# Norm boundaries of a two-layer encoder ordered by sequence, with the means spread by a product with ones, and a quarter of the first modulation moved to the vector engine

## What is computed

```python
for i in range(2):
    mod = silu(c) @ w_mod[i] + b_mod[i]            # 6 x 1024 columns per sequence
    sh1, sc1, g1, sh2, sc2, g2 = split(mod, 6)
    h = rmsnorm(x, norm1_g[i]) * (1 + sc1) + sh1
    mix = even_mixer(h) if i % 2 == 0 else odd_mixer(h)
    x = x + g1 * mix
    h = rmsnorm(x, norm2_g[i]) * (1 + sc2) + sh2
    x = x + g2 * ((silu(h @ w_g) * (h @ w_u)) @ w_down)
return rmsnorm(x, final_g)
# rmsnorm(x, g) = x * rsqrt(mean(x * x over the 1024 features) + eps) * g
```

## Time and profile before

| | |
|---|---|
| median of 3 runs | 2123.8 us (2117.55 to 2126.86) |
| profiled execution, own time | 2124.51 us |
| its span | 2122.4 us |
| mean granted clock of PE | 0.967 of full |
| PE busy | 2017.7 us (95%) |
| VectorE busy | 992.6 us (47%) |
| ScalarE busy | 601.7 us (28%) |
| chain that ended last, by engine | PE 87%, DVE 6%, ACT 4%, issue 2%, DMA 1% |

### The profile page before, as it was taken

The page is one execution under the profiler, slowest core; times in us unless marked ns, Lnnn a source line. Parts: engine busy times, 40 slices in busy tenths (PEclk is TensorE's granted clock), DMA queues, the critical chain, the costliest instruction groups (busy, mean ns, idle before and its releaser), DMA issues.

```text
span 2122.4 us, 28746 instructions
## 1 busy us (share of the span) xinstructions
PE 2017.7 (95%) x12081; PEld 1742.5 (82%) x12081; DVE 992.6 (47%) x1875; ACT 601.7 (28%) x1101; POOL 74.3 (4%) x121
## 2 busy tenths in 40 slices
PE   7879999988899999999998999998989999999998
PEld 2768888767788888888887788888878888888887
DVE  1877425684766665652235334544452222222224
ACT  3235224652321112211223333334232211211213
POOL 2010000000011101100000000000000000000000
PEclk9889999999899999999998999999989999999999
DMA  7343112012344444432223201021212222222212
GB/s 282 120 150 108 41 41 80 21 31 60 99 142 138 136 122 139 142 96 60 65 62 104 60 20 41 21 99 49 61 50 60 60 70 60 64 66 60 62 56 82
DMA packets 210249, 174.16 MB, mean 82 GB/s; under 512 B 10320, under 2 KB 196792, under 8 KB 208584
## 3 DMA queue, kind: packets, MB, share of 16 engines
q1 hardware_dynamic: 197536, 117.67, 18.5%
q0 software_dynamic: 12288, 48.35, 7.1%
q10 hardware_dynamic: 296, 6.29, 0.7%
HBM read 162.85 MB, written 9.44 MB: 81 GB/s over the span
## 4 chain that ended last, share of the span: by engine, by line
PE 87%; DVE 6%; ACT 4%; issue 2%; DMA 1%; POOL 0%; ACTq 0%; DVEq 0%; POOLq 0%
PE bank L824 60%; PE bank L790 9%; PE bank L842 4%; PE bank L1096 2%; PE bank L747 1%; PE bank L765 1%; DMA early_raw<-in_w_mod_dram 1%; ACT w_hi L1221 1%; DVE early_acc L1620 1%; DVE w_lo L1601 1%; PE bank L1018 1%; PE bank L908 1%; PE bank L1041 1%; PE bank L966 1%; PE bank L1068 1%
## 5 line engine op out<-in xcount | busy, mean ns | idle before, releaser
L824 PE MATMUL bank<-h_hi,w_hi 128*128 128x256 f32 x1600 | 409.4, 338 | 0.1
L824 PE MATMUL bank<-h_lo,w_hi 128*128 128x256 f32 x1600 | 407.5, 336 | 0.0
L824 PE MATMUL bank<-h_hi,w_lo 128*128 128x256 f32 x1600 | 407.3, 336 | 0.0
L1601 DVE TENSOR_TENSOR w_lo<-raw,w_hi 128x1024 fp32r<-128x1024 f32 (+4 forms) x195 | 239.0, 1230 | 340.2 <-ACT w_hi L1221 340.1
L824 PEld LDWEIGHTS bank<-h_hi,w_lo 128*128 128x128 f32 x1600 | 301.3, 188 | 33.6
L824 PEld LDWEIGHTS bank<-h_lo,w_hi 128*128 128x128 f32 x1600 | 301.4, 188 | 33.2
L824 PEld LDWEIGHTS bank<-h_hi,w_hi 128*128 128x128 f32 x1600 | 299.4, 188 | 34.2 <-issue 1.9
L1221 ACT ACTIVATE w_hi<-raw 128x1024 fp32r<-128x1024 f32 (+4 forms) x196 | 205.6, 1053 | 226.3 <-DMA raw<-in_ffn_w_down_dram 129.1
L790 PE MATMUL bank<-w_hi,h_hi 128*128 128x256 f32 x672 | 214.8, 320 | 18.1 <-DVE w_lo L1601 17.7
L790 PE MATMUL bank<-w_lo,h_hi 128*128 128x256 f32 x672 | 195.8, 291 | 0.0
L790 PE MATMUL bank<-w_hi,h_lo 128*128 128x256 f32 x672 | 195.6, 291 | 0.0
(11 more groups left out here) (274 smaller groups left out, 2251.7 us busy)
## 6 DMA issues: line engine op xcount, KB each, us to landing
raw<-in_ffn_w_gu_dram SPq DMA_DIRECT2D x176, 256.0 KB, 3.3
late_raw<-in_w_mod_dram POOLq DMA_DIRECT2D x56, 512.0 KB, 4.3
raw<-in_ffn_w_down_dram SPq DMA_DIRECT2D x64, 256.0 KB, 3.3
early_raw<-in_w_mod_dram POOLq DMA_DIRECT2D x24, 512.0 KB, 4.4
wide<-in_w_mod_dram SPq DMA_DIRECT2D x8, 1024.0 KB, 18.7
raw<-in_odd_w_in_dram SPq DMA_DIRECT2D x16, 512.0 KB, 4.4
raw<-in_even_w_in_dram SPq DMA_DIRECT2D x24, 256.0 KB, 5.0
x_kept<-x ACTq DMA_DIRECT2D x2, 3072.0 KB, 10.3
```

The costliest lines, as they stand in the source:

```text
L824: last = mm(pair(u.pair)[s], wk[a], seq(operand(o, k), s), start=(k == 0 and n == 0), stop=(k == u.ks - 1 and n == 2))
L1601: v.tensor_tensor(lo, r, hi.bitcast(F32), ALU.subtract).then_inc(unit_split, 1)
```

## The change

At every norm boundary inside the program the two sequences are taken one after the other, the wide one first.

- **Tail** (`tail_units`): the last two units of `outa0`, `down02` and `out1` are computed as unit 7 wide, unit 8 wide, unit 7 narrow, sums of the wide squares, unit 8 narrow. PE waits for both units' weights and banks before the first of them. Residuals and squares of these two units are per sequence.
- **Means**: `norm_sums(n, s)` multiplies a 128x128 matrix of ones by the squares themselves, three products as wide as the sequence, so that every partition of a bank holds the sum of every token. ACT takes the root straight from the bank, with the epsilon as a bias column, into `rstd_all` (128 x 768). DVE's reciprocal is over that tile: 128x512 and 128x256 in place of 128x6. The diagonals and their six products are gone.
- **Head** (`head_units`): three units instead of two: units 1 and 2 wide tile by tile, inside which (after the third tile) the narrow sums are made; unit 3 wide; then the three units narrow.
- **Splits**: the splits of the units that follow are placed inside the norm on ACT and DVE.
- **First modulation**: columns 0 to 511 of the 2048 are accumulated on DVE (`modulate_first` there, 128x512 per sequence and slice) and summed by PE with a column of ones; PE keeps three banks per slice. ACT's split of the first four units waits for slice 5 instead of slice 8. The distance table is made behind `lowrank0` instead of ahead of `norm(0)`. The spill of `norm(0)` and `norm(2)` is issued between the two sequences.

Pieces of the diff: PE's sums, PE's head, ACT's part of the norm, DVE's reciprocal, DVE's part of the start.

```diff
-            def norm_sums(n):
+            def norm_sums(n, s):
-                pe.wait_ge(sq_summed, (KD - 2) * (n + 1))
-                for t in range(TILES):
-                    mm(mean_bank(n)[:, t:t + 1], square_sum[:, t * P:(t + 1) * P], ones[:, 0:1], start=True, stop=True)
...
-                    mm(pair(2)[s][:, c:c + P], ones[:], rstd_diag[:, t, :], start=True, stop=True).then_inc(rstd_full, 1)
+                mm(mean_of(n, s), ones[:], seq(square_sum, s), start=True, stop=False)
+                for f in (KD - 2, KD - 1):
+                    pe.wait_ge(sq_ready, 10 * n + (7, 9)[1 - s] + f - (KD - 2))
+                    last = mm(mean_of(n, s), ones[:], seq(square[f % 2], s), start=False, stop=(f == KD - 1))
+            def head_units(us, n):
...
+                for k in range(KD):
+                    pe.wait_ge(h_ready, 2 * KD * n + k + 1)
+                    for u in us[:2]:
+                        products(u, 1, k)
+                    if n and k == 2:
+                        norm_sums(n, 0)
...
+                for f in range(KD):
+                    high(f, 1)
+                    if n and f == 1:
+                        square_late(KD - 1, 0, 4)
+                    if n and f == 3:
+                        mean_root(n, 0)
+                        split_to(us[KD - 2].i)
...
+            def inverse(n, s):
+                dve.wait_ge(root_ready, 2 * n + 2 - s)
+                link(v.reciprocal(seq(rstd_all, s), seq(rstd_all, s)))
...
+            inverse(0, 1)
+            inverse(0, 0)
+            modulate_first(KD - 1)
+            split_to(-1)
             dve.wait_ge(mod_full, KD)
```

More of the change, by code:

```diff
@@ L285, in build @@
         row_taken = sem("row_taken")
+        first_step = [sem(f"first_step{s}") for s in range(2)]
         hi_ready = sem("hi_ready")
@@ L401, in build @@
                 by = "act"
-            pairs = 3 if base in ("gu", "down") else 2
-            u.pair = (0 if u.n == 0 and pairs == 3 else features) % pairs
+            if u.tail is not None:
+                by = "res"
+                taken["res"] = 4 * u.tail + 2 + u.n - (KD - 2)
+            pairs = 3 if base in ("gu", "down") or u.name in HEADS and u.n < 3 else 2
+            u.pair = u.n if u.name in HEADS and u.n < 3 else (0 if u.n == 0 and pairs == 3 else features) % pairs
             features = u.pair + 1
@@ L475, in build, with mean_of @@
             splittable.setdefault(-1 if u.prior is None else u.prior, []).append(u)
-        def mean_bank(n):
-            return bank[6 if 0 < n < 4 else 0]
+        def mean_of(n, s):
+            if n == 0:
+                return pair(0)[s]
+            return bank[6][:] if s else bank[7][:, 256:512]
         def mod_column(l, c):
@@ L711, in _ @@
             pool.wait_ge(mod_full, KD)
+            for s in range(2):
+                pool.wait_ge(first_step[s], KD)
             mod_loads(0, EARLY)
@@ L851, in after, with tail_units @@
                     sum_mods(b)
[L853 to L858, removed]
+            def tail_units(us, n, operand):
+                for u in us:
+                    pe.wait_ge(unit_split, u.i + 1)
+                    wait_free(u)
+                for s in (1, 0):
+                    for u in us:
+                        if s == 0 and u is us[1]:
+                            if n == 2:
+                                pe.wait_ge(mod_ready, 1 + len(MOD_BLOCKS))
+                            norm_sums(n, 1)
+                        for k in range(u.ks):
+                            wk = [slot_of(wt, u)[:, k * P:(k + 1) * P] for wt in (w_hi, w_lo)]
+                            for m, (a, o) in enumerate(((0, 0), (0, 1), (1, 0))):
+                                last = mm(pair(u.pair)[s], wk[a], seq(operand(o, k), s),
+                                          start=(k == 0 and m == 0), stop=(k == u.ks - 1 and m == 2))
+                        last.then_inc(group_full, 1)
@@ L859, in feature_units @@
+            def feature_units(name, before=None, operand=normal, mix=None, head=None, tail=None):
                 us = phase[name]
+                if head is not None:
+                    head_units(us[:3], head)
+                    us = us[3:]
                 if before:
@@ L863, in feature_units @@
                     after(us[1])
-                for u in us[2 if before else 0:]:
+                    us = us[2:]
+                for u in us if tail is None else us[:-2]:
                     feature_tile(u, operand, None, mix)
                     after(u)
+                if tail is not None:
+                    tail_units(us[-2:], tail, operand)
             def down_units(l, g):
[L869 to L872, removed]
+                us = phase[f"down{l}{g}"]
+                for u in us:
+                    if u.tail is None:
+                        feature_tile(u, gated,
+                                     (lambda k: pe.wait_ge(act_ready, hidden_before[l, g] + k + 1)) if u.n == 0 else None)
+                        after(u)
+                if us[-1].tail is not None:
+                    tail_units(us[-2:], 2, gated)
             def token_units(us, mix):
@@ L1532, in feed_forward @@
                     run(phase[f"gu{l}{g}"], hidden(l, g))
-                    run(phase[f"down{l}{g}"], squares_of(2 * l + 2) if g + 1 == FG else take_nothing)
-            spill()
+                    run([u for u in phase[f"down{l}{g}"] if u.tail is None], squares_of(2 * l + 2) if g + 1 == FG else take_nothing)
             norm(0, 0)
```

311 lines of the change are left out of this document (208 added, 103 removed).

## The result

The change takes 2133.2 us in the median of 6 runs (2127.4 to 2137.1) against 2124.4 us of the kernel before in 6 runs (2117.6 to 2128.5): ratio 1.004, 95% interval 1.002 to 1.0059, which is 4 to 12.5 us longer. The profiled execution of the change took 2127.42 us, its span is 2125.7 us; that is 2.9 us above the profiled execution of before and the shortest of its six. The forecast was 2129 us, +4.3 on the profiled execution.

A forecast was written before the change was run, and what follows sets the result against it. PE, busy 95% of the span, bounds the kernel, but DVE sets the start. Start +1.5 and three norms +2.8 give +4.3 on the profiled 2124.5 us: 2129 us, range 2108 to 2140.

The forecast's parts named there:

- The wide reciprocal: DVE's reciprocal in the norm chain: 6.2 ns a column, 3.3 us wide and 1.75 us narrow, where 0.19 us stood.
- The pipelined rival: DVE's reciprocals take only 0.74 and 0.48 us, making the whole 2107 us; chance 0.18.
- The steeper rival: DVE's reciprocal costs 8.3 ns a column, 4.4 and 2.3 us, making the whole 2135.3 us; chance 0.20.
- steps 1 to 4: Norm 2: means at 13.1 us, first product 20.2, tile five ready 30.6, third unit's end 53.0 against 52.0, +1.0.
- step 2: Norm 2: root, reciprocal, scaling and splits to first product at 20.2 us; PE stands 4.9, then half clock for 5.6 us.
- Norm 1: Stretch from sixth unit to third unit behind the norm: 50.8 us, +0.3, with 1.14 us for the sixth unit's residual.
- Norm 3: Stretch from sixth unit to third unit behind the norm: 57.8 us, +1.6.
- The full-clock rival: PE's clock stays at full through the gap at the norms, making the whole 2119 us; chance 0.12.
- The start: First modulation and first norm: DVE's clock counts, norm ends 1.3 us early, but distance table and spill make it +1.5 us.
- PE's 7 us: At the start, the 7 us of modulation work saved on PE were said to shorten nothing.

The follow-up runs named there:

- act_inverse: Changed kernel with ACT making the inverse root in one operation, DVE's two reciprocals gone; 2107.9 us, ratio 0.9928 to the kernel before.
- Root_behind: Changed kernel with ACT's narrow root moved from behind the fourth wide tile to behind the seventh; 2119.3 us, ratio 0.9978 to the kernel before.
- keep_warm: Changed kernel with 18 products of ones by ones added on PE ahead of the head at norms 1 to 3; ratio 1.0089 to the kernel before.
- change_again: The changed kernel run once more, nothing altered; ratio 1.0044 to the kernel before, median 2130.6 us.
- Share0: Changed kernel with PE making all four banks of the first modulation again, DVE none; ratio 1.0048 to the kernel before.
- row_first: Changed kernel with DVE's row copy ahead of the four splits and PE's one-column sums ahead of the turns; ratio 1.0011 to the kernel before.
- before_a: The kernel before run once more, nothing altered, for a second trace; long matmul pairs cover 591 us of it, 11.0 us lost.

## Why the prediction was right, and where it was off

- **The wide reciprocal**: 3.3 and 1.75 us forecast, 3.35 and 1.75 measured, from the slope between 6 and 24 columns. The pipelined rival (2107 us) is refuted by this row. That act_inverse came out at 2107.9 us is a coincidence of the number: it has no reciprocal at all, where that rival kept 0.74 and 0.48 us, and it is 15 us under its own kernel before, where the rival gained 17.5. The steeper rival needed 8.3 ns a column; the rows show 6.25. The Trainium skill ("VectorE: DVE Perf Modes", First, the fixed hardware budget) gives the reciprocal a repeat count of 8; the trace (6.25 ns a column) lies under what 8 cycles a column would make of it, an estimate of 8.3 ns, and decides.
- **Norm 2, steps 1 to 4**, from the sixth unit's residual at 1115.2: means at 12.9 us (forecast 13.1), first product at 20.0 (20.2), PE's stand 4.95 (4.9), narrow sums at 28.1 (28.4), tile five ready for DVE at 30.2 (30.6), DVE's stand 5.49 (6.4), third unit's end at 52.5 (53.0). Root_behind and act_inverse show that the narrow root and the reciprocals carried time; the half clock of step 2 was there, but its price by itself no run isolates (keep_warm bounds it at some 2.5 us).
- **Norm 1** was off by 1.5 us in the profiled execution: the stand ahead of the tail was put at 1.14 us, the residual alone, and measured 2.48. The residual came at 521.00, 1.2 us behind PE's end of that unit, since a split and a square sum stood ahead of it in DVE's list; and behind this stand the granted clock was 0.50 from 524 to 526, for which the forecast had no term. In change_again the stand was 1.51 us, the clock stayed at 1.00, and the stretch was 50.8 us, the forecast.
- **Norm 3** took 56.1 us in one trace and 57.5 in the other (forecast 57.8). Behind the same stand of 4.07 us the lower clock lasted about 3 us in the one and 6 us in the other. Windows of the change and then of change_again, from the first product on:

```profile
1547.00:1549.00 2.00, 1.76 (x4) 1.51 (x5) 1.97 (x4) 1.14 (x2) 0.00 (x0) 0.50 0.00 0
1549.00:1551.00 2.00, 2.00 (x8) 1.56 (x7) 1.97 (x4) 0.72 (x1) 0.00 (x0) 0.74 0.00 0
1551.00:1553.00 2.00, 2.00 (x11) 1.65 (x10) 1.11 (x2) 0.00 (x0) 0.00 (x0) 1.00 0.04 8
```

```profile
1549.00:1551.00 2.00, 1.81 (x4) 1.49 (x5) 1.96 (x4) 1.14 (x2) 0.00 (x0) 0.50 0.00 0
1551.00:1553.00 2.00, 2.00 (x6) 1.57 (x5) 1.96 (x4) 0.72 (x1) 0.00 (x0) 0.50 0.00 0
1553.00:1555.00 2.00, 2.00 (x6) 1.52 (x6) 1.07 (x2) 0.00 (x0) 0.00 (x0) 0.51 0.03 8
```

- **The full-clock rival** is wrong: behind 4.07, 4.95 and 5.51 us of standing the clock was 0.50 each time. In act_inverse, behind stands of 0.69 to 2.13 us, it was 1.00.
- **The start**: forecast +1.5, measured +1.66 at PE's first product of bv0; the first scaling at 60.8 forecast, 61.05 measured. One sentence of it was too strong: that PE's 7 us "reach nobody". Share0 shows that 3 of them arrive; the rest of the start took more than that back. Of that rest, row_first shows the row copy behind four splits and the order of the sums (3.5 us); the distance table and the half clock under the one-column sums (0.50 from 56 to 60) are in the trace, but no run prices them.
- **The stretches that the change doesn't touch** were put at nothing. In the profiled pair they cancel to about a microsecond: from 130 us to the sixth unit 2.4 us shorter, the two feed-forwards 2.1 us longer each, the odd mixer 4.1 us shorter, the last norm 1.6 us longer (its 12 sums took 2.72 us at the lower clock). That the profiled pair, at +2.9, came so close to +4.3 is in part luck: these stretches cancel, and so do norm 1 (1.5 us over its forecast) and norm 3 (1.7 under). In the medians they do not: start and norms make 4.1 us in the profiled pair, and 5.1 us between the means of the traces in the table, of the 8.8. The term that was missing is the one of the next section, 2.1 us behind each feed-forward head; that it is the whole rest is argued from traces of single executions, not shown.

So the mechanism held step by step, and the median came out 4 us above the forecast, inside the range, for a reason that had no step and is not shown in full.

## What to carry to other kernels

A wait in an engine's list is paid by everything behind it: the root of the second half, made where it was convenient, cost 11 to 14 us, and moving that one line won more than the reordering had lost. Ahead of a reordering that spreads a statistic over many columns, price each operation of the chain at the new width by the longest pair of rows of the same operation, since operations of one engine can differ several times over (here 6.25 ns a column for the reciprocal, and (742 - 480) / 256 = 1.0 for the scaling). And when a chain of small operations is shortened, look for the engine that can make two steps in one: the inverse root on ACT took 5.1 us a norm off DVE, for two more table loads of 1.28 us on ACT in the whole program.

## What the runs showed that was not expected

The products of one unit alternate between 256 and 512 columns. Of one and the same program, a pair of matmuls takes 0.3467 us in some blocks and 0.3533 us in others at a granted clock of 1.00, for ten to over three hundred microseconds at a time. Groups of PE by form (count, busy us, mean ns), from 1600 to 1680, in the profiled execution of before:

```profile
L824 PE MATMUL bank<-h_hi,w_hi 128*128 128x512 f32 x78 | 30.5, 391 | 0.0
L824 PE MATMUL bank<-h_lo,w_hi 128*128 128x512 f32 x77 | 30.1, 391 | 0.0
L824 PE MATMUL bank<-h_hi,w_lo 128*128 128x512 f32 x77 | 30.1, 391 | 0.0
```

in before_a:

```profile
L824 PE MATMUL bank<-h_hi,w_hi 128*128 128x512 f32 x76 | 30.6, 403 | 0.0
L824 PE MATMUL bank<-h_lo,w_hi 128*128 128x512 f32 x76 | 30.2, 398 | 0.0
L824 PE MATMUL bank<-h_hi,w_lo 128*128 128x512 f32 x76 | 30.0, 395 | 0.0
```

and in the change:

```profile
L856 PE MATMUL bank<-h_lo,w_hi 128*128 128x512 f32 x76 | 30.6, 403 | 0.0
L856 PE MATMUL bank<-h_hi,w_hi 128*128 128x512 f32 x76 | 30.0, 395 | 0.0
L856 PE MATMUL bank<-h_hi,w_lo 128*128 128x512 f32 x75 | 29.9, 398 | 0.0
```

Three means of 391 ns, or one each of 403, 398 and 395, which falls to another product from one trace to the next. The second feed-forward takes 527.1 us in two traces of before and 533.0 in the third; in the change and its variants 529.2 where the first block alone is slow and 533.0 to 533.4 where more is. In the blocks right behind the heads of the two feed-forwards all eleven traces of the change and its variants run slowly, 22 places of 22 (by the pairs from 590 to 670 and from 1595 to 1680), of the kernel before 1 of 6. What starts it, and why the new heads always leave PE in it, stays open; a wait of PE for its own last product does not end it. By the count given under before_a it costs 4 to 15 us of an execution, as much as several of the effects studied here. It does not alone make one execution differ from the next: the profiled execution of before at 2124.5 us lost 3.9 us by it, the one at 2118.3 us lost 5.6.
